# Rotary row exchange of the mLSTM queries and keys by transfers inside SBUF, and the gate columns in one unit

## The reference, cut to what matters

```python
p = h @ w_in + b_in
(mq, mk, mv, mo, mi, mf, ...) = jnp.split(p, ...)      # 4 heads x 128 each; mi, mf: 8 columns each
if latent:
    mq, mk = rope_2d(mq), rope_2d(mk)                  # only the 512 latent tokens
ig = mi;  lf = log_sigmoid(mf + ml_fbias)
h_ml = mlstm_bidir(mq, mk, mv, ig, lf, c0, n0, m0)

def rope_1d(x, pos):                                   # on 64 of the 128 rows of a head at a time
    x1, x2 = x[..., :32], x[..., 32:]
    return concatenate([x1 * cos - x2 * sin, x1 * sin + x2 * cos])
```

## Time and profile before

| what | us |
|---|---|
| three runs: lowest, median, highest | 3090.0, 3101.82, 3114.78 |
| the profiled execution, its own time | 3102.25 |
| span of its trace | 3100.5 |
| layer 0: last query unit ends, last value tile ends | 81.66, 162.31 |
| layer 1: last query unit ends, last value tile ends | 1639.54, 1721.69 |

### The profile page before, as it was taken

How to read it: one execution, slowest core, us unless ns; L and a number is a source line. 1 busy time by engine, 2 the same in 40 slices (tenths; PEclk the granted TensorE clock), 3 DMA queues, 4 the chain that set the end, 5 groups by cost and what they waited for, 6 DMA issues and landing times.

```text
span 3100.5 us, 42428 instructions
## 1 busy us (share of the span) xinstructions
PE 2933.6 (95%) x17662; PEld 2395.2 (77%) x17662; DVE 1798.1 (58%) x2079; ACT 1374.1 (44%) x1775; POOL 545.9 (18%) x218
## 2 busy tenths in 40 slices
PE   5999989999998999999989999899999799999998
PEld 4969878898986676767669798899999567666665
DVE  3651334324437989888865422351342698989797
ACT  3043320111127777776750433310110677777775
POOL 2414313133220000000024133142332100000000
PEclk8989989999998999999999899899999899999999
DMA  8513547457436989898985134332443398989896
GB/s 237 84 28 69 100 116 200 126 160 177 98 114 217 351 283 348 279 336 279 348 232 81 29 58 93 76 69 41 82 82 116 120 351 289 340 288 347 287 326 237
DMA packets 357648, 580.76 MB, mean 187 GB/s; under 512 B 13712, under 2 KB 148880, under 8 KB 357328
## 3 DMA queue, kind: packets, MB, share of 16 engines
q1 hardware_dynamic: 297488, 501.26, 55.2%
q10 hardware_dynamic: 51808, 56.53, 5.7%
q0 software_dynamic: 8160, 20.26, 2.0%
HBM read 568.54 MB, written 9.45 MB: 186 GB/s over the span
## 4 chain that ended last, share of the span: by engine, by line
PE 84%; DVE 6%; DMA 4%; ACT 2%; issue 2%; DVEq 1%; SPq 1%; ACTq 0%; POOL 0%; POOLq 0%
PE ps L838 28%; PE ps L1327 10%; PE ps L1330 10%; PE ps L1335 10%; PE ps L802 6%; PE ps L882 3%; PE ps L1244 2%; DMA ring<-w_down 2%; PE ps L1108 2%; DVE w_lo L2279 1%; PE ps L914 1%; PE ps L1025 1%; PE ps L864 1%; PE ps L1009 1%; DMA arena<-ada_w 1%
## 5 line engine op out<-in xcount | busy, mean ns | idle before, releaser
L2279 DVE TENSOR_TENSOR w_lo<-ring,w_hi 128x2048 fp32r<-128x2048 f32 x256 | 584.0, 2287 | 94.2 <-ACT w_hi L1457 93.5
L838 PE MATMUL ps<-h_hi,w_hi 128*128 128x320 f32 x1792 | 560.9, 313 | 8.3 <-DVE mod L2328 3.8
L838 PE MATMUL ps<-h_hi,w_lo 128*128 128x320 f32 x1792 | 556.0, 310 | 0.0
L838 PE MATMUL ps<-h_lo,w_hi 128*128 128x320 f32 x1792 | 555.9, 310 | 0.0
L1457 ACT ACTIVATE w_hi<-ring 128x2048 fp32r<-128x2048 f32 x256 | 486.9, 1909 | 74.1 <-DMA ring<-w_up 24.1
L678 POOL CAST w_hi<-ring 128x2048 fp32r<-128x2048 f32 (+1 forms) x76 | 142.8, 1879 | 1558.1 <-DMA ring<-w_in 1005.1
L1520 ACT ACTIVATE arena<-ps,par 128x640 f32<-128x640 f32 x88 | 70.0, 796 | 695.5 <-PE ps L838 672.5
L838 PEld LDWEIGHTS ps<-h_hi,w_hi 128*128 128x128 f32 x1792 | 338.7, 189 | 16.7 <-issue 7.1
L680 POOL TENSOR_TENSOR w_lo<-ring,w_hi 128x2048 fp32r<-128x2048 f32 (+1 forms) x76 | 345.6, 4547 | 28.0 <-issue 27.4
L838 PEld LDWEIGHTS ps<-h_lo,w_hi 128*128 128x128 f32 x1792 | 338.7, 189 | 0.5 <-issue 0.5
L838 PEld LDWEIGHTS ps<-h_hi,w_lo 128*128 128x128 f32 x1792 | 338.2, 189 | 0.0
(11 more groups left out here) (320 smaller groups left out, 5350.2 us busy)
## 6 DMA issues: line engine op xcount, KB each, us to landing
ring<-w_gate SPq DMA_DIRECT2D x128, 1024.0 KB, 5.8
ring<-w_up SPq DMA_DIRECT2D x128, 1024.0 KB, 6.3
ring<-w_down SPq DMA_DIRECT2D x128, 1024.0 KB, 7.0
ring<-w_in SPq DMA_DIRECT2D x64, 1024.0 KB, 13.3
arena<-ada_w ACTq DMA_DIRECT2D x40, 1024.0 KB, 5.7
arena<-ada_w SPq DMA_DIRECT2D x8, 1024.0 KB, 18.0
arena<-biasT ACTq DMA_DIRECT2D x16, 512.0 KB, 6.2
ring<-w_o SPq DMA_DIRECT2D x8, 1024.0 KB, 16.4
```

Of the source, the lines that this page charges most:

```text
L838: last = pe.matmul(ps[:, bank(u) + half, 0:HALF], w[:, k, f0:f0 + P], a[:, k, at], start=(k == 0 and part == 0), stop=(k == KD - 1 and par ...
L2279: dve.tensor_tensor(w_los[g % NW], ring[:, s, :], w_his[g % NW].bitcast(F32), ALU.subtract).then_inc(slot_used[s], 1)
```

## The change

**Row exchange.** The rotation products on PE and their 8 units go. After the read-out of every second head ACT issues four transfers (`swap_rows`), each copying 32 partitions, 2 heads and 512 latent tokens from `mq` or `mk` into `rot_q` or `rot_k` with the quadrants of 32 partitions exchanged; a pair of heads is 4 x 128 KB, and there are 4 pairs in a layer. Before it issues a pair it waits for its own read-out and for the pair before to have landed. `rope` on DVE waits for the transfers of a pair, multiplies `rot` by sin in place (the table has the sign now), and goes on as before.

**Gate columns.** A weight tensor `w_if` is laid out on the host with the input gate in columns 0 to 7 and the forget gate in columns 32 to 39 of 128, so that one chunk, one split and one unit serve both; DVE reads partitions 0 to 7 and 32 to 39 of that unit. An unused unit of kind "none" keeps the banks of the later units where they were. All later chunks of the layer move down by one in the ring and in the order of the splits, which changes the parity of the two split buffers.

**Tables.** In layer 1 the reload of sin and cos counts on `params_in`, for which both ACT (ahead of the read-out of the queries) and DVE wait.

```diff
-(R_MQ, R_G, R_MK, R_MV, R_MO, R_NQ, R_NK, R_NV) = range(0, 16, 2)
+R_MQ, R_G = 0, 2
+(R_MK, R_MV, R_MO, R_NQ, R_NK, R_NV) = range(3, 15, 2)
...
-        rope_tmp = view(W_AT + 2560, TS)
+        rot_q, rot_k = view(W_AT + 2560, HM, TS), view(5120, HM, TS)
...
-        U_MQ, U_RQ = unit("act", HM), unit("dve", HM)
-        U_G = unit("dve", 2)
-        U_MK, U_RK = unit("act", HM), unit("dve", HM)
+        U_MQ = unit("act", HM)
+        U_G = unit("dve", 1)
+        unit("none", 1)
+        U_MK = unit("act", HM)
...
+        ends[R_G] = U_G
         for j in range(2):
-            ends[R_G + j] = U_G + j
...
+        def last_split(b):
+
+            return MIX_SPLITS - 1 - (MIX_SPLITS - 1 - b) % 2
...
-                return split_used(l, MIX_SPLITS - 2 + g)
+                return split_used(l, last_split(g))
...
-                for j in range(2):
-                    load(l, R_G + j, rows_of(win_l, C_G + 8 * j, GC))
+                load(l, R_G, rows_of(w_if[l, :, :], 0, GC))
...
-                    pool.dma_start(cst[:, K_COS:K_COS + 2 * TS], const[:, K_COS:K_COS + 2 * TS]).then_inc(cos_back.sem, 16)
+                    pool.dma_start(cst[:, K_COS:K_COS + 2 * TS], const[:, K_COS:K_COS + 2 * TS]).then_inc(params_in.sem, 16)
...
-                split(l, R_G)
+                split(l, R_G, 1)
...
-                while l and v >= 0 and units[v] == "ada":
+                while v >= 0 and (units[v] == "none" or l and units[v] == "ada"):
...
-            def rope_rows(l, u0, src, first):
-                for i in range(HM):
-                    free_unit(l, u0 + i)
-
-                    pe.wait_ge(*emptied(l, u0 - HM + i))
-                    pe.matmul(ps[:, bank(u0 + i), :], rotate, src[:, i, TP:T], start=True, stop=True)\
-                        .then_inc(unit_full.sem, 1)
...
                 project(l, R_MQ, range(U_MQ, U_MQ + KB), fresh=True)
-                rope_rows(l, U_RQ, mq, 0)
-
-                for j in range(2):
-                    b, hi, lo = split_chunk(l, R_G + j, GC)
-                    split_unit(l, U_G + j, hi, lo, 0)
+
+                b, hi, lo = split_chunk(l, R_G, GC)
+                split_unit(l, U_G, hi, lo, 0)
                 project(l, R_MK, range(U_MK, U_MK + KB))
-                rope_rows(l, U_RK, mk, HM)
                 project_tokens(l, R_MV, U_MV)
...
+            def swap_rows(l, pair, u, src, rot):
+
+                act.wait_ge(*emptied(l, u))
+                if pair:
+                    act.wait_ge(*rot_in.at(l, 4 * pair))
+                heads = slice(2 * (pair % 2), 2 * (pair % 2) + 2)
+                for quadrant in range(4):
+                    to, of = 32 * quadrant, 32 * (quadrant ^ 1)
+                    act.dma_start(rot[to:to + 32, heads, :], src[of:of + 32, heads, TP:T])\
+                        .then_inc(rot_in.sem, 16)
...
-                act.wait_ge(*params_in.at(l, 4))
+                act.wait_ge(*params_in.at(l, 4 + min(l, 1)))
                 for i in range(HM):
                     empty(l, U_MQ + i, mq[:, i, :], bcol(B_MQ + i))
+                    if i % 2:
+                        swap_rows(l, i // 2, U_MQ + i, mq, rot_q)
...
                     empty(l, U_MK + i, mk[:, i, :], bcol(B_MK + i))
+                    if i % 2:
+                        swap_rows(l, 2 + i // 2, U_MK + i, mk, rot_k)
...
-            def rope(l, u0, dst):
+            def rope(l, first, dst, rot):
                 for i in range(HM):
-                    dve.wait_ge(*filled(l, u0 + i))
-                    dve.tensor_tensor(rope_tmp, ps[:, bank(u0 + i), :], sinT, ALU.mult).then_inc(dve_emptied.sem, 1)
+                    pair = first + i // 2
+                    dve.wait_ge(*rot_in.at(l, 4 * (pair + 1)))
+                    dve.tensor_tensor(rot[:, i, :], rot[:, i, :], sinT, ALU.mult)
                     dve.tensor_tensor(dst[:, i, TP:T], dst[:, i, TP:T], cosT, ALU.mult)
                     dve.drain()
-                    dve.tensor_tensor(dst[:, i, TP:T], dst[:, i, TP:T], rope_tmp, ALU.add).then_inc(roped.sem, 1)
+                    dve.tensor_tensor(dst[:, i, TP:T], dst[:, i, TP:T], rot[:, i, :], ALU.add).then_inc(roped.sem, 1)
                     dve.drain()
 
             def gate_rows(l):
-                dve.tensor_scalar(rbias[:, :], rowpar[:, 1:2], rowpar[:, 2:3], None, ALU.add)
+                dve.tensor_scalar(rbias[32:40, :], rowpar[32:40, 1:2], rowpar[32:40, 2:3], None, ALU.add)
                 dve.memset(row_zero[0:8, :], 0.0)
                 dve.drain()
                 dve.wait_ge(*filled(l, U_G))
-                dve.tensor_scalar(cols(row_ig[0:8, :]), ps[0:8, bank(U_G):bank(U_G) + 2, 0:HALF], rowpar[:, 0:1],
-                                  None, ALU.add).then_inc(dve_emptied.sem, 1)
-                b = bank(U_G + 1)
-                dve.wait_ge(*filled(l, U_G + 1))
-                dve.tensor_scalar(cols(row_lf[0:8, :]), ps[0:8, b:b + 2, 0:HALF], rbias[:, :], None, ALU.add)\
+                b = bank(U_G)
+                dve.tensor_scalar(cols(row_ig[0:8, :]), ps[0:8, b:b + 2, 0:HALF], rowpar[0:8, 0:1], None, ALU.add)
+                dve.tensor_scalar(cols(row_lf[0:8, :]), ps[32:40, b:b + 2, 0:HALF], rbias[32:40, :], None, ALU.add)\
                     .then_inc(dve_emptied.sem, 1)
...
-                dve.wait_ge(*params_in.at(l, 4))
+                dve.wait_ge(*params_in.at(l, 4 + min(l, 1)))
                 dve.tensor_scalar(gq[:, :], par[:, Q_GQ:Q_GQ + 1], DN ** -0.5, None, ALU.mult)
                 dve.drain()
-                if l:
-                    dve.wait_ge(*cos_back.at(l - 1, 1))
-                rope(l, U_RQ, mq)
+                rope(l, 0, mq, rot_q)
                 gate_rows(l)
-                rope(l, U_RK, mk)
+                rope(l, 2, mk, rot_k)
...
-            k[at:at + 32, K_SIN:K_SIN + TS] = np.sin(ang)
+            k[at:at + 32, K_SIN:K_SIN + TS] = np.sin(ang) if s else -np.sin(ang)
...
-    rowp = np.stack([b_in[:, C_G:C_G + 8], b_in[:, C_G + 8:C_G + 16], fm, m0], axis=2)
+    rowp = np.zeros((DEPTH, 40, 4), f32)
+    rowp[:, 0:8] = rowp[:, 32:40] = np.stack([b_in[:, C_G:C_G + 8], b_in[:, C_G + 8:C_G + 16], fm, m0], axis=2)
+    w_if = np.zeros((DEPTH, D, GC), f32)
+    w_if[:, :, 0:8], w_if[:, :, 32:40] = a["w_in"][:, :, C_G:C_G + 8], a["w_in"][:, :, C_G + 8:C_G + 16]
```

More of the change, by code:

```diff
@@ L87 @@
 MIX_SPLITS = len(SPLITS)
-assert MIX_SPLITS % 2 == 0
 RING_LAYER = R_EXP + FFN_CHUNKS
@@ L135, in at, with step_program @@
         return self.sem, (l * self.per_layer + k) * self.unit
-def step_program(nc, xT, cond, const, prm, rowp, biasT, ckT, cv, c0, ada_w, w_in, w_pa, w_pb, w_pc,
+def step_program(nc, xT, cond, const, prm, rowp, biasT, ckT, cv, c0, w_if, ada_w, w_in, w_pa, w_pb, w_pc,
                  w_o, w_router, w_gate, w_up, w_down, yT, new_k, new_v, new_cn, new_m, nv_dram, x_dram):
@@ L172, in step_program @@
         par = sb("par", [P, NPRM])
-        rowpar = sb("rowpar", [8, 4])
+        rowpar = sb("rowpar", [40, 4])
         cond_in = sb("cond_in", [P, KD, 2])
@@ L186, in step_program @@
         gq = sb("gq", [P, 1])
-        rbias = sb("rbias", [8, 1])
+        rbias = sb("rbias", [40, 1])
         wend = sb("wend", [P, 8])
@@ L372, in step_program @@
         acol_ready = signal("acol_ready", 1)
+        rot_in = signal("rot_in", 16, 16)
         roped = signal("roped", 2 * HM)
@@ L426, in step_program @@
         wp_ready = signal("wp_ready", 12)
-        cos_back = signal("cos_back", 1, 16)
         merged_ready = signal("merged_ready", 24)
@@ L513, in step_program @@
         dve_before = [sum(1 for k in units[:u] if k == "dve") for u in range(len(units) + 1)]
-        full_before = [sum(1 for k in units[:u] if k != "ada") for u in range(len(units) + 1)]
+        full_before = [sum(1 for k in units[:u] if k not in ("ada", "none")) for u in range(len(units) + 1)]
         unit_full.per_layer = full_before[-1]
@@ L672, in split @@
                     s = ring_slot(l, q)
-                    n = KD * GC if R_G <= q < R_G + 2 else CHUNK
+                    n = KD * GC if q == R_G else CHUNK
                     pool.wait_ge(slot_landed[s], (ring_uses(l, q) + 1) * 16)
@@ L1863, in gate_rows @@
                         dve.tensor_tensor_scan(rowM[0:8, d, order], row_lf[0:8, order], row_ig[0:8, order],
-                                               rowpar[:, 3:4] if g else 0.0, ALU.add, ALU.max)
+                                               rowpar[0:8, 3:4] if g else 0.0, ALU.add, ALU.max)
                 dve.drain()
@@ L2496 @@
         "cv": a["cache_ctx_v"][0].reshape(DEPTH, P, WB),
-        "c0": a["state_mlstm_c"][0].reshape(DEPTH, 8, P, P),
+        "c0": a["state_mlstm_c"][0].reshape(DEPTH, 8, P, P), "w_if": w_if,
         **{n: a[n] for n in ("ada_w", "w_in", "w_pa", "w_pb", "w_pc", "w_o", "w_router", "w_gate", "w_up", "w_down")},
```

## The result

The changed kernel takes 3086.39 us (median of 11 runs, 3076.89 to 3087.94), the kernel before 3106.6 (11 runs, 3090.0 to 3118.99). The ratio is 0.9926 with a 95% interval of 0.9907 to 0.9944: a gain of some 20 us, within 1%. The forecast was 3069.0 with a range from 3055 to 3089. The time lies in the range, 17 us above the forecast. Four of these 17 are the starting point: the forecast starts from 3102.25, the median of the kernel before was 3106.6 in these runs. By the medians 20.2 of the predicted 33.3 us were won, and the question is where the other 13 went. The profiled execution took 3084.54 us, with a span of 3082.8.

A forecast was written before the change was run, and what follows sets the result against it. PE, busy 95% of the span, was taken to bound the kernel. The stage saves 33.8 us in both layers, less 0.5 of waits ahead of the keys: 3102.25 - 33.3 = 3069.0 us, range 3055 to 3089.

The forecast's parts named there:

- own signs of being wrong: PE waiting on DVE in the keys or ahead of value tile 4, or a later stage giving the time back.
- late transfers: Rival, chance 0.13: row-exchange transfers share DMA engines with a ring load and land in 14.3 to 18.9: 3073 to 3089.
- The stage: Last query unit to last value tile: 64.5 us after the change, removing 16.15 in layer 0 and 17.65 in layer 1.
- The second query pair: Issued by 84, landing at 90; landing by 96 costs nothing, each microsecond later costs PE one at the third key unit.
- DVE stopped by GpSimd: DVE operations with two SBUF inputs stop while GpSimd works, 4.92 against 0.69; the change makes such lines three.
- Split of the first key chunk: Ahead of the keys, PE waits 0 to 0.6 for this split; 0.25 a layer taken, 0.5 in all.
- key pairs: Both landed by 126, value tile 0 read out at 135.7, needed at 140: slack 4.5 us, no cost.
- layer 1's table: Sin and cos reload lands at 1621.0, ahead of ACT's read-out at 1624.68: hidden with 3.7 to spare.
- Whole loads ahead: Rival, chance 0.06: a pair's packets stand behind up to two ring loads, landing after 24.4: 3111 and more.
- At nothing: Items costed at zero: one 512 KB load and one small split less, ring's shift, split parity, SP's queue.
- The ring's shift: Later chunks of the layer moving down one ring slot: costed at nothing.
- what follows the stage moves forward as it is: Everything behind the changed stage was to start earlier with its length unchanged, giving none of the gain back.

The follow-up runs named there:

- early read-out: Changed kernel, with DVE reading the gate unit out between the two query pairs instead of after both: ratio 0.9933 to the kernel before.
- combination: Changed kernel with w_if declared last, two convolution loads held until the last bias transfer landed, and the gate unit read out between the query pairs: ratio 0.9867.
- gate columns alone: Kernel before plus only the single gate unit with its new weight input in front; rotation products stay on PE: ratio 1.0027.
- before with the shift: Kernel before with an unused 1 MB input put ahead of ada_w, no instruction changed: 3111.3 us, ratio 1.002.
- held value chunks: Changed kernel, with SP holding layer 0's two value chunk loads until the first and second query pair have landed: ratio 0.9933 to the kernel before.
- exchange alone: Kernel before plus only the row exchange by transfers; the two gate units stay: ratio 0.9935.
- input last: Changed kernel with w_if declared behind all other inputs, same instructions: 3061.9 us, ratio 0.9883 to the kernel before.
- gate columns with input last: Kernel before plus only the single gate unit, rotation left on PE, its weight input declared behind all others: ratio 0.9973.
- 2 MB further: Changed kernel with an unused 1 MB input behind w_if, so ada_w, w_in and all behind lie 2 MB further than before: ratio 0.9875.
- held convolution loads: Changed kernel, with SP holding the fifth and sixth convolution chunk loads until the layer's last bias transfer has landed: ratio 0.9877 to the kernel before.

## Why the prediction was right or wrong

*The range and the signs.* The time came out in the range, which is 34 us wide, but two of the prediction's own signs of being wrong appeared: PE waited on DVE in the keys (in layer 0), and a stage behind gave time back. That the sum still fitted the range is in part luck. 3086 lies in the band of the late transfers (3073 to 3089), yet these cost 7.3 us, in one layer; the rest has a cause that no rival named.

*The stage.* Right in layer 1 to 0.4 us (64.1 for 64.5): the gate unit, eight rotary products, the wait and the fall of the clock went, and nothing took their place. In layer 0 the time of the stage is 64.5 only where the first pair lands early or DVE reads the gate unit out early.

*The second query pair.* The mechanism was named and its chain was the right one: the third key unit waits for DVE's read-out of the gate unit, which is queued behind the rope of the second pair. The term was mis-sized, in three steps. First, the pair was taken to be issued by 84. In the trace it is issued from 85.21 to 87.13, because ACT waits for the first pair's landing before it issues the second (`if pair: act.wait_ge(*rot_in...)`), and that landing was 14.55 behind the issue in a stretch where loads keep the DMA share at 0.93. The wait is in the diff; I priced the two landings each by itself and not one behind the other. Second, the landing at 98.3 was to cost 2.1. DVE needed 8.7 from there to the end of the read-out and not 7.0, since GpSimd's next split stopped one more sum (L1845, 2.22 below), and PE stood ready at 101.4 and not 103.1, since its stage began 1.5 earlier than before: 5.7. Third, the clock that fell behind the wait added 2.0. The first landing of 14.55 and the second of 11.16 lie in the bounds of 3.7 and 18.9 taken from the earlier trace rows; the 6.2 that I took is nearer to the transfers' median (3.6 in layer 0) than to these two, and these two are the ones that count.

```profile
85.15 2.41 DVE L1842 TENSOR_TENSOR arena<-arena,cst 128x512 f32<-128x512 f32 x1 [26.90 <-DMA arena<-arena]
87.49 2.38 DVE L1843 TENSOR_TENSOR arena<-arena,cst 128x512 f32<-128x512 f32 x1
89.94 4.96 DVE L1845 TENSOR_TENSOR arena<-arena 128x512 f32<-128x512 f32 x1
94.99 0.69 DVE L1842 TENSOR_TENSOR arena<-arena,cst 128x512 f32<-128x512 f32 x1
...
98.31 0.69 DVE L1842 TENSOR_TENSOR arena<-arena,cst 128x512 f32<-128x512 f32 x1 [1.26 <-DMA arena<-arena]
...
101.84 2.22 DVE L1845 TENSOR_TENSOR arena<-arena 128x512 f32<-128x512 f32 x1
```

*DVE stopped by GpSimd.* Right: a sum took 4.96 us while GpSimd's subtraction ran (89.48 to 94.35), a product with `rot` 2.41 beside the subtraction before it (to 87.02) and one with cos 2.38 beside the cast between them; they took 0.69 otherwise. This is the rule of the Trainium skill (SBUF — State Buffer, Who interferes with whom) that the prediction weighed, and the trace after agrees with it in all three lines. In layer 1 PE did not notice.

*Split of the first key chunk, key pairs, layer 1's table.* Right: PE's largest wait ahead of the keys is 0.5 in all the kernels with the exchange, and in these kernels it waits for DVE at the last value tile in two executions only, the early read-out (0.8) and the combination (3.8), in layer 0. In layer 1 PE waits nowhere over 0.2 from the queries to the values.

*Whole loads ahead.* Did not come. The longest landing was 14.55 us, where two loads ahead were to give 24.4. While the first pair flew, packets of both queues went in each slice, as between 73 and 76 (q1 has SP's loads, q10 ACT's transfers; packets, MB, share of the 16 engines):

```profile
q1 hardware_dynamic: 356, 0.36, 94.6%
q10 hardware_dynamic: 51, 0.08, 10.0%
```

That is in line with the rule of the Trainium skill (DMA: Bandwidth & Descriptors, Queues, rings and completion order) that the queues are served packet by packet in turn, now for copies inside SBUF too. Equal turns it doesn't show: seven of SP's packets went for one of ACT's.

*At nothing, and what follows.* This is the step that failed. "The ring's shift" was rightly nothing: the input's place alone, with ring and parity as in the change, brings 0.9883. But "what follows the stage moves forward as it is" was wrong, and not by a new wait: the new tensor moved `w_in` and all behind it by 1 MB, and loads that fly together land later. In the twelve stretches of attention, two a kernel, with the input in front (after twice, gate columns alone, before with the shift, early read-out, held value chunks) the two loads took 17.0 to 19.7 us; in the twelve without it or with 2 MB (before twice, exchange alone, input last, gate columns with input last, 2 MB further) 12.7 to 16.3, and the slowest bias transfer 18.6 to 21.6 in the first and 11.6 to 15.6 in the second. Attention of both layers together is 217.7 to 224.8 in the first and 200.1 to 215.1 in the second. By the ratios the input's place cost the changed kernel 0.0043 (13 us), where 0.0033 were missing (0.9926 for 0.9893); by medians over their own runs of before 0.0063 (20 us), where 13 us were. So it is worth what was missing or more.

Attention is not the only place. Behind attention of layer 0 PE waits once for a transfer of `ada_w`, which moved too (after, then input last):

```profile
PE ps L910 <- DMA arena<-ada_w: 6.3, 1, 6.3
```

```profile
PE ps L910 <- DMA arena<-ada_w: 2.9, 1, 2.9
```

This wait is 6.1 to 7.6 in the seven executions with 1 MB in front (the held convolution loads among them) and 2.4 to 3.8 in the seven others, so it accounts for some 3.5 of the 7.7 us that the piece between the layers lost.

*The sum.* 33.3 us were predicted, a ratio of 0.9893. With the input last it is 0.9883, 2 MB further 0.9875. That the two meet is partly chance: against the mean of the two spans before, the execution with the input last won 13.2 and 18.0 up to the transposes, and a further 7.9 in attention, which the prediction did not claim.

*What stays open.* Why one megabyte matters and two don't: only shifts of 0, 1 and 2 MB were tried, and the profile shows no addresses: that inputs lie in memory in the order in which they are declared is taken for granted. The place of `w_in` against the bias table, which did not move, is not what matters: held until no bias transfer is in flight, the two loads took 20.0 and 18.0 us with the input in front and 15.0 and 15.6 with the input last, in layer 1 with nothing else in flight. Whether the shift slows the kernel before was not settled (1.002, 0.9992 to 1.0047). The piece between the layers varies from 1145 to 1163. The shift orders it in part: 1150.3 to 1159.8 in the six executions with the input in front, 1145.1 to 1150.0 in five of the six others, but 1155.5 with the exchange alone and 1162.7 with all together. What it holds beyond the wait for `ada_w` I can't place.

## What to carry to other kernels

A change that adds, drops or resizes a tensor in device memory can move every tensor behind it: declare new inputs last, or compare the landing times of the loads that did not change before looking for a cause in the instructions. Where transfers are chained by waits on one queue, price the last one from the landing of those ahead of it, in the busiest stretch, and not from its own median. A short engine chain that becomes late because PE arrives earlier (the gate unit alone) turns a gain on PE into a wait, so the two halves of a change are worth timing apart.

## What the runs showed of the hardware

Two loads of 1 MB beside bias transfers landed in 12.7 to 16.3 us on the mean or in 17.0 to 19.7, by a shift of their source by 1 MB in the order of the inputs; a shift of 2 MB gave the former. With no bias transfer in flight the two took 15.6 and 18.0 (layer 1). Behind a wait of PE of 5.7 us the granted clock was 0.53 and 0.61 in the next two stretches of 4 us, and 96 matmuls took 2.0 more; behind waits of 2.2 (input last, 2 MB further) they took 1.7 more, behind one of 1.6 they took 14.32. A transfer of 128 KB inside SBUF landed in 2.3 us at best and in up to 14.5 beside the loads (after, layer 0), and its issue cost ACT 0.59 to 1.64 us, where an issue of ACT's bias transfers cost 0.37:

```profile
L1524 ACTq DMA_DIRECT2D arena<-arena x16: 592/620/1639, 66.9 to 126.0; - x16
...
DMA to landing us min/median/max: 2.3/3.6/14.5
```
